# Last units of two output projections by token halves, and work moved between and within engines in a two-block transformer kernel

## The reference

```
x = x + even_layer(x)        # RMS norm, w_in, conformer convolution and block attention, gates, w_out
x = x + odd_layer(x)         # RMS norm, w_in, low-rank queries, an indexer's top-64 keys, attention, w_out
x = rms_norm(x, final_norm)  # "the norm of the first block"
h = rms_norm(x, g_mix_2)     # "the third norm" of the kernel
q, k, v, z, f, scal, gates = split(h @ w_in_2)
y_a = gated_deltanet(q, k, v, z, scal)   # 8 heads, forward and backward, chunks of 64
y_f = fourier(f)
x = x + (gate_a * y_a + gate_f * y_f) @ w_o_2
x = x + square(relu(rms_norm(x, g_mlp_2) @ w_mlp_up_2)) @ w_mlp_down_2
out = rms_norm(x, g_final_2)
```

## Time and profile before

| | |
|---|---|
| runs | 2228.39, 2230.98, 2231.80 us, median 2230.98 us |
| profiled execution, its own time | 2229.79 us |
| its span (first to last instruction) | 2228.0 us |
| mean granted TensorE clock | 0.997 of 2.4 GHz |
| PE busy | 2183.3 us, 98% |
| POOL, DVE, ACT busy | 1714.7 us (77%), 1075.7 us (48%), 1026.2 us (46%) |
| HBM read | 380 MB, 171 GB/s over the span |

### The profile page before, as it was taken

One profiled execution on the slowest core, in us unless ns is written; L12 is line 12 of the kernel. 1 busy time (PEld: TensorE's weight loads), 2 busy tenths in 40 slices (PEclk: granted clock), 3 DMA queues, 4 the chain that ended last, 5 costly groups with the idle time before them and its releaser, 6 DMA issues.

```text
span 2228.0 us, 34192 instructions
## 1 busy us (share of the span) xinstructions
PE 2183.3 (98%) x12563; PEld 1872.0 (84%) x12563; DVE 1075.7 (48%) x1812; ACT 1026.2 (46%) x1432; POOL 1714.7 (77%) x721
## 2 busy tenths in 40 slices
PE   8999999999999999999999999999999999999997
PEld 7888888888888878888888888888888888888886
DVE  4994243115863142557574835316704813822831
ACT  5434455454456554535354644444333343333343
POOL 7888858887666966657575758888888888888885
PEclk9999999999999999999999999999999999999999
DMA  7666545655454754445454646665656666656654
GB/s 232 189 189 190 180 140 166 186 158 173 133 151 137 242 153 142 135 131 161 124 161 115 169 122 191 206 191 184 190 193 190 189 196 189 189 192 194 189 190 142
DMA packets 321440, 383.86 MB, mean 172 GB/s; under 512 B 14654, under 2 KB 255781, under 8 KB 321061
## 3 DMA queue, kind: packets, MB, share of 16 engines
q1 hardware_dynamic: 317237, 377.80, 56.0%
q10 hardware_dynamic: 4080, 4.33, 0.6%
HBM read 379.98 MB, written 2.10 MB: 171 GB/s over the span
## 4 chain that ended last, share of the span: by engine, by line
PE 88%; DVE 6%; POOL 2%; issue 2%; ACT 1%; DMA 1%; ACTq 0%; POOLq 0%; DVEq 0%
PE lin_ps L2100 33%; PE lin_ps L2103 16%; PE lin_ps L2135 9%; PE lin_ps L2137 9%; PE lin_ps L2136 9%; POOL w_lo L619 2%; DVE ps L1786 2%; ACT w_hi L647 1%; PE ps L2577 1%; PE lin_ps L2280 0%; PE ps L2064 0%; PE ps L2425 0%; PE lin_ps L2282 0%; PE lin_ps L2281 0%; DVE own L1927 0%
## 5 line engine op out<-in xcount | busy, mean ns | idle before, releaser
L619 POOL TENSOR_TENSOR w_lo<-raw,w_hi 128x1024 fp32r<-128x1024 f32 x716 | 1714.4, 2404 | 494.1 <-ACT w_hi L647 387.2
L2100 PE MATMUL lin_ps<-a,w_hi 128*128 128x512 f32 x2176 | 700.1, 403 | 4.9 <-POOL w_lo L619 4.5
L647 ACT ACTIVATE w_hi<-raw 128x1024 fp32r<-128x1024 f32 x456 | 478.0, 1058 | 471.4 <-PE lin_ps L2103 253.0
L2103 PEld LDWEIGHTS lin_ps<-a,w_lo 128*128 128x128 f32 x2176 | 409.2, 188 | 96.5
L2100 PE MATMUL lin_ps<-b,w_hi 128*128 128x512 f32 x1376 | 433.0, 396 | 4.2 <-DVE z L1458 2.2
L2103 PE MATMUL lin_ps<-a,w_lo 128*128 128x256 f32 x2176 | 428.7, 278 | 0.0
L658 ACT ACTIVATE w_hi<-raw 128x1024 fp32r<-128x1024 f32 x228 | 242.1, 1062 | 384.5 <-PE lin_ps L2103 225.3
L2100 PEld LDWEIGHTS lin_ps<-a,w_hi 128*128 128x128 f32 x2176 | 334.1, 189 | 14.2 <-POOL w_lo L619 6.2
L2103 PEld LDWEIGHTS lin_ps<-b,w_lo 128*128 128x128 f32 x1376 | 258.5, 188 | 61.1
L2135 PE MATMUL lin_ps<-w_hi,a 128*128 128x512 f32 x768 | 299.6, 390 | 0.0
L2137 PE MATMUL lin_ps<-w_hi,a 128*128 128x512 f32 x768 | 298.9, 389 | 0.0
(11 more groups left out here) (415 smaller groups left out, 2121.5 us busy)
## 6 DMA issues: line engine op xcount, KB each, us to landing
raw<-in_w_in SPq DMA_DIRECT2D x144, 512.0 KB, 3.7
raw<-in_w_mlp_up SPq DMA_DIRECT2D x128, 512.0 KB, 3.7
raw<-in_w_mlp_down SPq DMA_DIRECT2D x128, 512.0 KB, 3.6
raw<-in_even_w_in SPq DMA_DIRECT2D x112, 512.0 KB, 3.7
raw<-in_odd_w_in SPq DMA_DIRECT2D x40, 512.0 KB, 3.6
raw<-in_even_w_out SPq DMA_DIRECT2D x32, 512.0 KB, 4.1
raw<-in_odd_w_out SPq DMA_DIRECT2D x32, 512.0 KB, 4.8
raw<-in_w_o SPq DMA_DIRECT2D x32, 512.0 KB, 4.2
```

The lines of the kernel that those rows point to most:

```text
L619: nc.gpsimd.tensor_tensor(w_lo[:, slot], raw[:, slot], w_hi[:, slot].bitcast(F32), ALU.subtract).then_inc(lo_done, 1)
L647: nc.scalar.activation(w_hi[:, slot], raw[:, slot], ACT.Copy).then_inc(hi_done, 1)
L2100: nc.tensor.matmul(lin_ps[:, 2 * parity + m, :], hi[:, k, m * P:(m + 1) * P], src[:, kk].rearrange("p s n -> p (s n)"), start=(q == 0 and ...
L2103: last = nc.tensor.matmul(lin_ps[:, 2 * parity + m, 0:T], lo[:, k, m * P:(m + 1) * P], src[:, kk, 0, :], start=False, stop=(q == n - 1 and ...
```

## The change

1. **By token halves.** In `odd_w_out` and `mlp3` the last four units of the last column block run in two passes: all four for q = 0 (counted in a new semaphore `half_done`), then all four for q = 1 (each then counts as used). `to_x_gains` handles q = 0 after the first pass, calls a function for those tokens, and only then waits for q = 1. For the third norm this function is the sum, root, reciprocal and the two first scaled copies of q = 0; at the end it is q = 0's reciprocal and all its output scaling. The one-line sums are made per token half (`rest_of_both`). SP sends both DMAs of q = 0 first. ACT scales blocks 0 and 1 of q = 1 and DVE blocks 2 and 3. ACT converts the third norm's units 0 and 1 after q = 0's root (the three first ones stood before the norm) and unit 2 between its scaled copies and `upper(0)`. PE turns blocks 0 and 1 by q first.
2. **Even layer.** A dummy exponential (`prime(0)`) stands before round 0's exponentials; the gate's silu goes behind round 0's next two conversions, followed by another dummy. In round 3 the reciprocals come before `even_out(25)`.
3. **Top-k mask.** The selected mask goes to PSUM (`kept`) and the two adds read it from there.
4. **Key eviction.** ACT, not DVE, writes the turned keys back, and converts that unit, before the round's exponentials.
5. **DeltaNet.** ACT's `fill(6)` stands before `silus(other)`, and the next ones each one place earlier; DVE sets `w.inv` after both convolutions; PE's two `grams` and two `spread` follow each other; one half unit is put behind level 6.

```diff
@@ projections, PE
+            def by_tokens(name, src):
+                u0, g0 = OUTS[name]
+                for q in range(TT):
+                    acc = lin_ps[:, 2 * ((g0 + NB - 1) % 2) + q, :]
+                    for j in range(4, 8):
+                        u = u0 + 8 * (NB - 1) + j
+                        if q == 0:
+                            pe.wait_ge(lo_done, u + 1)
...
+                        if q:
+                            last.then_inc(unit_used, 1)
+                        elif j == 7:
+                            last.then_inc(half_done, 1)
@@ normed, PE
-                for n in range(2):
-                    turn_block(r, n)
+                for q in range(TT):
+                    for n in range(2):
+                        pe.wait_ge(nm_sc[q].sem, nm_sc[q].at(f"{n}", SCALED[r]))
...
@@ to_x_gains, DVE
+                before_last()
+                dve.wait_ge(half_done, rnd + 1)
+                add(NB - 1, 0)
+                gain(NB - 1, 0)
+                after_first()
+                dve.wait_ge(unit_used, u0 + 8 * NB)
+                add(NB - 1, 1)
+                gain(NB - 1, 1)
+            def rest_of_both(q):
+                dve.wait_ge(mg_rs.sem, mg_rs.at("c2"))
+                nc.vector.scalar_tensor_tensor(out=nst[:, 32 + q:33 + q], in0=sq_sum[:, ...], scalar=1.0 / D,
+                                               in1=nst[:, 28 + q:29 + q], ...)
+                dve.wait_ge(mg_rs.sem, mg_rs.at(f"t{q}"))
+                nc.vector.scalar_tensor_tensor(out=rest[:, q:q + 1], in0=nst[:, 32 + q:33 + q], scalar=EPS, ...)
+            def first_tokens():
+                rest_of_both(0)
+                first_half()          # reciprocal of q = 0, scale(0), scale(1)
+            to_x_gains("odd_w_out", 0, 2, rests, first_tokens)
+            rest_of_both(1)
+            second_half()             # reciprocal of q = 1, lower(0), scale(2), ...
@@ third norm, ACT
-            for j in range(6, 35):
+            for j in range(6, 32):
...
             for q in range(TT):
+                added_squares(0, 2, OUTS["odd_w_out"][1], NB - 1, (q,))
+                squares2(NB - 1, (q,))
...
+                if q == 0:
+                    for j in (32, 33):
+                        hi(u0 + j, (u0 + j) % SLOTS)
@@ norm, ACT
                 scale(0)
                 scale(1)
+                hi(u0 + 2, (u0 + 2) % SLOTS)
                 upper(0)
@@ end, SP, ACT, DVE
-            for n in range(2):
-                for q in range(TT):
+            for q in range(TT):
+                for n in range(2):
...
-            for n in (0, 1, 3):
+            for n in range(2):
...
+            for n in (2, 3):
+                nc.vector.tensor_scalar(x[:, 1, _block(n)], x[:, 1, _block(n)], recip[:, 1:2], None, ALU.mult)
@@ even layer, ACT and DVE
                 his_up(done_to + 1, first + 2)
                 if r == 0:
-                    act.wait_ge(group_free, 22)
-                    gate = z[:, Z_BGATE:Z_BGATE + 8, :]
-                    nc.scalar.activation(gate, gate, ACT.Silu).then_inc(ev_act.sem, 1)
+                    prime(0)
...
                 his_up(first + 3, first + 4)
+                if r == 0:
+                    act.wait_ge(group_free, 22)
+                    gate = z[:, Z_BGATE:Z_BGATE + 8, :]
+                    nc.scalar.activation(gate, gate, ACT.Silu).then_inc(ev_act.sem, 1)
+                    prime(1)
...
+                both(e_sums, r)
                 if r == 3:
                     even_out(25)
-                both(e_sums, r)
@@ mask and keys
-            nc.vector.tensor_scalar(work, work, -3.2e38, -1.0e30, ALU.is_ge, ALU.mult)
+            nc.vector.tensor_scalar(kept, work, -3.2e38, -1.0e30, ALU.is_ge, ALU.mult)    # kept = ps[:, 1, :]
...
+                if r in (0, 1, 3):
+                    act.wait_ge(od_pe.sem, od_pe.at(f"ukt{j}"))
+                    act.wait_ge(group_free, g)
+                    nc.scalar.activation(raw[:, u % SLOTS], lin_ps[...], ACT.Copy).then_inc(group_free, 1)
+                    ahead_to = first + 2
+                    his_to(ahead_to, ahead_to)
@@ DeltaNet, ACT then PE
-                fill(5)
+                fill(5, 6)
                 silus(other)
-                fill(6)
+                fill(7)
                 norms(one_way)
-                fill(7)
+                fill(8)
                 norms(other)
-                fill(8)
...
                 grams(one_way)
-                fill(2)
                 grams(other)
-                fill(6)
+                fill(9)
                 spread(one_way)
-                fill(4)
                 spread(other)
-                fill(10)
+                fill(12)
...
-                for l, ready, n in ((4, None, 2), (5, "u4", 2), (6, "l53", 0)):
+                for l, ready, n in ((4, None, 2), (5, "u4", 2), (6, "l53", 1)):
```

169 lines of the change are left out of this document (100 added, 69 removed).

## The result

The changed kernel takes 2214.1 us (median of four runs, 2212.95 to 2215.47), the one before 2230.9 us (2228.39 to 2231.80): ratio 0.9928, 95% interval 0.9916 to 0.9940, which is 16.8 us or 0.75% less. The forecast was 2218.4 with a range of 2211 to 2225.

A forecast was written before the change was run, and what follows sets the result against it. PE's matmuls, busy 2183.3 of 2228.0 us, were taken as the floor. Terms 2.8 + 1.9 − 1.0 + 6.3 + 2.6 = 12.6 us won gave 2217.2 from 2229.8, or 2218.4 against the median; range 2211 to 2225.

The forecast's parts named there:

- Even layer, 2.8 forecast: Even layer: exponentials start earlier in round 0 (1.3 us), reciprocals go ahead of evictions in round 3 (1.5); 2.8 won.
- Odd rounds, 1.9 forecast: Odd heads: mask's adds reading PSUM win 1.5 us, the keys' eviction on ACT 0.4; 1.9 won.
- the hold of the second negation: Odd rounds: DVE's second negation, an SBUF instruction, is held by POOL's conversion for up to 2.0 us.
- Third norm, 1.0 lost forecast: Third norm: halves win 0.2 us with q = 1's sum held, the longer low clock costs 1.2; 1.0 lost.
- DeltaNet, 6.3 forecast: DeltaNet pairs, four passes: waits on ACT's late conversion (3.7 us), `turn` waits (1.8) and PE's returns (0.8) go; 6.3 won.
- the returns: DeltaNet: merged grams and spreads save eight returns of PE to the projection, some 0.1 us each; 0.8 won.
- End, 2.6 forecast: End of program: with halves only 1 MB is left for the last DMA pair; 2.6 us won, bounds 0 and 3.5.
- A: Rival: DeltaNet's waits only move to the next late unit, giving 2.2 us instead of 6.3; 2222.5 us; chance 0.12.
- B: Rival: POOL doesn't hold DVE in the new places; third norm 3 us better, odd heads 1.4; 2214; chance 0.12.
- C: Rival: slower, DVE's chain in the DeltaNet pairs becomes the bound; 2235 us if DVE is 8 us late; chance 0.03.
- D: Rival: nothing gained at the places meant, each wait followed by one of equal length; 2229 to 2231; chance 0.04.
- The last unit's low part: Both ends, first half pass: wanted 0.4 us after it is ready; if late, both ends would cost some 1 us each.

The follow-up runs named there:

- d3: Kernel before with only `w.inv` set behind both convolutions and the mask in PSUM; 2224.2 us, ratio 0.9973.
- c5: Changed kernel with the third norm sums' constant input in PSUM, mask back in SBUF, silu back ahead of round 0's exponentials; 2216.4 us, ratio 0.9935.
- a1: Changed kernel with whole units and the old order back at the third norm only; 2213.5 us, ratio 0.9922.
- c2: Kernel before with only DeltaNet conversions 6 to 8 one place earlier and even round 3's reciprocals ahead of the eviction; 2223.6 us, ratio 0.9968.
- c3: Kernel before with only grams together, spreads together and one half unit behind level 6; 2227.7 us, ratio 0.9990.
- a2: Changed kernel with whole units and the old order of scaling and output DMAs back at the end; 2218.3 us, ratio 0.9945.
- a3: Changed kernel with ACT's DeltaNet conversions 6 to 8 back in their later places; 2216.0 us, ratio 0.9935.
- a4: Changed kernel with grams and spreads apart again and no half unit behind level 6; 2217.3 us, ratio 0.9941.
- c1: Changed kernel with `w.inv` back ahead of the convolutions and the keys' eviction back on DVE; 2215.7 us, ratio 0.9932.
- c4: Changed kernel with q = 1's third-norm sums on ACT and both attention layers' row maxima written to PSUM; 2209.0 us, ratio 0.9903.
- d1: c4 with 14 extra unread matmuls between the transposes of q = 0 and q = 1 at the third norm; 2205.7 us, ratio 0.9889.
- e1: d1 with three more extra matmuls behind q = 1's transposes and unit 2's conversion behind `upper(0)`, at the third norm; 2205.2 us, ratio 0.9887.

## Why the prediction held, point by point

The time lies in the range, 4.3 us below the forecast. The direction and most of the mechanisms were right. In DeltaNet, nearly half of the gain, the price came near by luck: one wait was read wrongly, one term is worth nothing, and one that was put at nothing carries 2.8 us.

**Even layer, 2.8 forecast.** Measured 1.35 in round 0 (forecast 1.3) and 1.56 in round 3 (1.5), less 0.25 for the late conversion behind the silu, which I had taken as hidden: 2.7.

**Odd rounds, 1.9 forecast.** The mask is worth 1.45 (1.5) by d3; c5's 1.74 has the low clock in it. The eviction on ACT 0.85 + 0.11, of which 0.4 was forecast; the hold of the second negation in rounds 0 and 3 came as said. Without it there would be 1.65 more (I had said 1.0 each). In all 2.4.

**Third norm, 1.0 lost forecast.** The hold came exactly: the sum held until POOL's second conversion ends. Before the first product the halves win 0.68 (9.23 to 8.55; 0.2 was forecast, since my estimate of the chain behind the sum was half a us too long). The clock takes it back: from the first product to a fixed instruction behind it, the kernels with whole units need 10.5 to 11.7 us and those with the halves, the sums on DVE and no other edit there 11.8 to 13.1, with the same work. Their means over five kernels each (before, a1, c2, c3, d3; after, a2, a3, a4, c1) are 11.3 and 12.2: 1.0 lost, 1.2 forecast. The clock's rows agree: the low stretch reaches 1.8 us behind the first product in the mean of the first five and 3.9 in the second, and 2.2 us more at half speed are 1.1. One profiled execution can't tell more, as the low stretch lasted about 3.4, 6.8 or 10.2 us in kernels of equal code. Net 0.2 to 0.3 lost.

**DeltaNet, 6.3 forecast, 7.8 measured.** Here steps failed, and the errors partly cancelled. I took L2594 for a line of `turn`, held up because "DVE is behind by `inv`". It is `first_solve`, which came right behind level 6 and waited for the one DVE step between; DVE had been idle before it, and 1.8 us stay in d3 and c2, with `inv` or the conversion moved. The half unit behind level 6, of which I wrote that it "moves work, it adds none", covers that wait and gives all of c3's 2.8 us. I had priced nothing for it, and 0.8 for the returns; no run shows a cost of returns, and the positions in c3 and a4 put it at nothing. `inv` sits at the head of the other path, that of the late conversion, and alone gives 4.0 us there. The conversion's move alone gives 4.9, not 3.7, and each adds little beside the other (1.07 and 0.16), the former in the first pass alone. The sum is then 5.0 for that path and 2.8 for the half unit.

**End, 2.6 forecast.** 2.81 by a2. The profile shows 3.38 (11.80 to 8.42); 0.57 of it lies between kernels with the same code at the end, 11.23 in a2 against 11.79 to 11.81 in before, c2, c3 and d3. Up to the first output DMA they are alike (3.91 to 3.93 us behind PE's end); from there to the end it takes 6.93 us in a2 and 7.48 to 7.50 in the four. So the difference is in the writing. What makes it stays open.

**The rivals.** A (the waits only move) is out: POOL's wait fell to 1.2 us. B (no hold) is out by mechanism, and yet its 2214 is the measured time: the pairs' 1.5, the end's 0.8, 0.5 in the odd rounds, 0.7 at the third norm and the swing of `w_out`, 0.7, add up to the same. The number alone would have confirmed the wrong rival. C is out: no wait at L2687, the line of `first_solve` after, is left. D is out. The last unit's low part was not late in the half passes: PE's waits have none at L2225 to L2227.

The measured parts sum to 2.7 + 2.4 - 0.3 + 7.8 + 2.8 = 15.4; of the remaining 1.4 of 16.8, 0.7 are the swing of `w_out` and 0.6 the end's difference in writing, in the profiled executions. That the medians differ by as much is not explained.

## What to carry to other kernels

Before costing two edits apart, write down the chain of engines that each one shortens: `inv` and the conversion lay on the same one, so their prices didn't add, and the wait that I put down to `inv` lay on another. Before naming a wait's cause, look at what its releaser did just before: DVE was idle there. A piece of other work put right behind a step whose result comes back through another engine can be worth more than the edits around it (0.7 us a pass for one half unit). If two edits share a kernel and a stage, read the trace piece by piece, since the run alone can't tell them apart. If POOL streams all the time, look for short DVE instructions whose duration differs from place to place; put one operand into PSUM, and it is 0.16 us everywhere, or give the instruction to ACT (together 5 us of this kernel). Where PE must stand still between two projections, the matmuls behind it can pay as well: shortening the chain by 0.9 us gave 0.4 (c4, less than the swing of this stage), filling the gap with matmuls that nobody reads 0.5 (d1), and e1's two edits 0.9 by the chain and 1.3 behind it.

## What the runs showed of the hardware

Some DVE instructions with only SBUF operands are held until the running POOL conversion ends: a two-column negation (TENSOR_SCALAR) 2.18 instead of 0.17 us, a one-column sum (SCALAR_TENSOR_TENSOR) 1.63 instead of 0.15. Others were not held beside POOL: a reciprocal 0.16 us (c5), a maximum over 512 columns 0.69, as without POOL. One input in PSUM was enough to free the held ones, even with another input in SBUF (c5, 0.14 us).

The granted clock fell to 0.50, 1.2 GHz, around a wait of PE of 4.4 us, and in d1 around one of 1.6 us; behind waits of 1.8 us in the odd rounds it fell in c5 and not in the kernel before. At the third norm it stayed at 1.00 in e1, where the longest wait there was some 0.3 us. With the low clock the transposes of q = 1 took 1.97 us, in e1 1.27, and two first matmuls 1.19 against 0.70. With the same code at this place the low stretch lasted 6.8 us and once 3.4 (whole units) or 10.2 (halves), and the stage differed by up to 1.5 us.

The start, where PE waits for the first loads, and the odd `w_out`, where ACT's conversions wait for theirs, vary by 3.3 and 1.9 us between the profiled executions with the same code there; the other stages of the table but the third norm, and the time behind the last matmul, repeat within 0.1 us. Of the 2.2 ms, the stretch between the last DeltaNet pass and the last matmul, 814.14 us, is the same in all fourteen.
